# Last feed-forward chunks reordered (four up products, then three down products), and the weight of the final norm multiplied in earlier

## What is computed

```python
h = h + merged @ w_out
hid = causal_dwconv(rms_norm(h, ffn_norm_g) @ w_ffn_up, ffn_conv_w, ffn_conv_b)   # width 3
g_ff, up = jnp.split(hid, 2, axis=-1)                                            # 2816 each
h = h + (jax.nn.silu(g_ff) * up) @ w_ffn_down                                    # 2816 -> 1024
out = h * lax.rsqrt(jnp.mean(h * h, axis=-1, keepdims=True) + 1e-6) * final_norm_g
```

## Time and profile before

| | us |
|---|---|
| median of 3 runs | 727.36 |
| the profiled execution's own time | 725.45 |
| its span, first to last instruction | 723.6 |
| TensorE busy in the span | 694.6 (96%) |
| VectorE busy | 495.7 (69%) |
| ScalarE busy | 372.6 (51%) |
| GpSimd busy | 14.9 (2%) |

### The profile page before, as it was taken

The page is one execution under the profiler, slowest core; times in us unless marked ns, Lnnn a source line. Parts: engine busy times, 40 slices in busy tenths (PEclk is TensorE's granted clock), DMA queues, the critical chain, the costliest instruction groups (busy, mean ns, idle before and its releaser), DMA issues.

```text
span 723.6 us, 13986 instructions
## 1 busy us (share of the span) xinstructions
PE 694.6 (96%) x5478; PEld 676.2 (93%) x5478; DVE 495.7 (69%) x626; ACT 372.6 (51%) x469; POOL 14.9 (2%) x26
## 2 busy tenths in 40 slices
PE   5898889999999999999999999999999999999994
PEld 5898889999999999999999999999999999999993
DVE  4893798878775656766754445655668777777784
ACT  5544787767663445454443333442465555455531
POOL 0000000000010000000000000000000000000021
PEclk9999999999999999999999999999999999999997
DMA  8729784739635544335555755556546555555511
GB/s 251 218 60 316 232 259 135 252 117 301 192 117 175 174 153 138 118 117 173 175 175 176 232 174 175 174 175 212 166 134 212 178 175 188 204 186 174 174 58 58
DMA packets 118170, 127.90 MB, mean 177 GB/s; under 512 B 4302, under 2 KB 113279, under 8 KB 117631
## 3 DMA queue, kind: packets, MB, share of 16 engines
q1 hardware_dynamic: 118143, 127.54, 55.0%
HBM read 126.43 MB, written 2.67 MB: 178 GB/s over the span
## 4 chain that ended last, share of the span: by engine, by line
PE 82%; DVE 8%; DMA 3%; ACT 2%; issue 2%; SPq 2%; DVEq 0%; POOL 0%; POOLq 0%; ACTq 0%
PE ps L339 26%; PE ps L341 26%; PE ps L340 26%; DVE w_lo L311 3%; DMA acs_b<-acs_d 2%; DVE conv_a L1214 2%; DMA w_raw<-w_in 1%; DVE conv_g L1497 1%; PE ps L626 1%; ACT decay L920 1%; PE ps L645 0%; PE ps L661 0%; PE ps L611 0%; PE ps L654 0%; DVE conv_o L1221 0%
## 5 line engine op out<-in xcount | busy, mean ns | idle before, releaser
L339 PE MATMUL ps<-tok_hi,w_hi 128*128 128x256 f32 x1056 | 302.7, 287 | 4.9 <-DVE w_lo L311 4.2
L341 PE MATMUL ps<-tok_hi,w_lo 128*128 128x256 f32 x1056 | 300.4, 284 | 0.0
L340 PE MATMUL ps<-tok_lo,w_hi 128*128 128x256 f32 x1056 | 300.3, 284 | 0.0
L311 DVE TENSOR_TENSOR w_lo<-w_raw,w_hi 128x2048 fp32r<-128x2048 f32 x107 | 244.8, 2289 | 73.4 <-ACT w_hi L307 73.2
L307 ACT ACTIVATE w_hi<-w_raw 128x2048 fp32r<-128x2048 f32 x108 | 206.2, 1910 | 58.5 <-PE ps L341 43.4
L339 PEld LDWEIGHTS ps<-tok_hi,w_hi 128*128 128x128 f32 x1056 | 204.3, 193 | 7.5 <-DVE w_lo L311 4.6
L340 PEld LDWEIGHTS ps<-tok_lo,w_hi 128*128 128x128 f32 x1056 | 204.3, 193 | 0.4
L341 PEld LDWEIGHTS ps<-tok_hi,w_lo 128*128 128x128 f32 x1056 | 204.2, 193 | 0.0
L339 PE MATMUL ps<-os_hi,w_hi 128*128 128x256 f32 x128 | 36.3, 284 | 0.0
L341 PE MATMUL ps<-os_hi,w_lo 128*128 128x256 f32 x128 | 36.2, 283 | 0.0
L340 PE MATMUL ps<-os_lo,w_hi 128*128 128x256 f32 x128 | 36.2, 283 | 0.0
(11 more groups left out here) (274 smaller groups left out, 1154.5 us busy)
## 6 DMA issues: line engine op xcount, KB each, us to landing
w_raw<-w_in SPq DMA_DIRECT2D x95, 512.0 KB, 4.8
w_raw<-w_ffn_up SPq DMA_DIRECT2D x44, 512.0 KB, 4.4
w_raw<-w_ffn_down SPq DMA_DIRECT2D x22, 512.0 KB, 4.0
w_raw<-w_mem_kv SPq DMA_DIRECT2D x16, 512.0 KB, 4.0
w_raw<-w_br_ssm SPq DMA_DIRECT2D x16, 512.0 KB, 4.3
acs_b<-acs_d SPq DMA_DIRECT2D x4, 1024.0 KB, 7.0
w_raw<-w_br_attn SPq DMA_DIRECT2D x8, 512.0 KB, 4.4
w_raw<-w_br_mem SPq DMA_DIRECT2D x8, 512.0 KB, 4.1
```

The source lines that it names most:

```text
L311: dve.tensor_tensor(w_lo[:, s, :], w_raw[:, s, :], w_hi[:, s, :].bitcast(F32), ALU.subtract).then_inc(lo_ready[s], 1)
L339: pe.matmul(o, a[0], b[0], start=start, stop=False, **kw)
L340: pe.matmul(o, a[0], b[1], start=False, stop=False, **kw)
L341: return pe.matmul(o, a[1], b[0], start=False, stop=stop, **kw)
```

## The change

The last two chunks (9 and 10) are taken out of the loops. The order on TensorE after chunk 8's step becomes gate 9, up 9, gate 10, up 10, down 8, down 9, down 10. The blocks are loaded in the same sequence of slots as before; what is in four of them differs. `ffn` of chunk 10 reads its gate product from slot 2 and its up product from slot 0. Chunk 9's hidden parts go to `last_hi` and `last_lo`, chunk 10's to two new tiles `end_hi` and `end_lo`, at places in memory that are free by then. The last down block is split by VectorE, between `hid` and `end_lo`, and GpSimd's split is gone.

In the final norm VectorE multiplies each quarter by the weight right after its addition, into `h_sc` (four new instructions), while ScalarE squares into a tile of its own (`junk_y`). GpSimd has three small instructions for each row tile in place of four. The last multiplication is by the column alone: VectorE does the right half of each row tile and ScalarE the left half. VectorE's first such multiplication stands after the third quarter and ahead of the fourth addition. ScalarE's first stands after the second square and ahead of the third. The right half is written out first.

```diff
--- before.py
+++ after.py
@@ -64,6 +64,7 @@
 BIAS_W = 3 * P
 
 RA, RB, RC, RD, RE, RF, RG = 0, 8, 12, 16, 20, 24, 26
+RL = RG + F_STEPS - 2
 DT_STEPS = 19
 
 
@@ -206,6 +207,9 @@
     gain_fin = place("gain_fin", R + 44, [D])
     last_hi = place("last_hi", R + 20, [2, T], F32R)
     last_lo = place("last_lo", R + 22, [2, T], F32R)
+    end_hi = place("end_hi", R + 48, [2, T], F32R)
+    end_lo = place("end_lo", R + 50, [2, T], F32R)
+    junk_y = place("junk_y", R + 52, [NT, D // 2])
     rstd_b = place("rstd_b", R + 18.5, [T])
     pad_g = place("pad_g", R + 0, [2, FTAPS - 1 + T])
     pad_u = place("pad_u", R + 2.25, [2, FTAPS - 1 + T])
@@ -272,8 +276,8 @@
               "h_lo"))
     pads_zero, conv_begun, f_step, g_tanh, g_silu, hid_done, hid_hi_s, hid_lo_s = map(
         sem, ("pads_zero", "conv_begun", "f_step", "g_tanh", "g_silu", "hid_done", "hid_hi_s", "hid_lo_s"))
-    down_done, y_added, y_sumsq, y_var, y_rstd, y_scaled, y_out = map(
-        sem, ("down_done", "y_added", "y_sumsq", "y_var", "y_rstd", "y_scaled", "y_out"))
+    down_done, y_added, y_gained, y_sumsq, y_var, y_rstd, y_left, y_right, y_out = map(
+        sem, ("down_done", "y_added", "y_gained", "y_sumsq", "y_var", "y_rstd", "y_left", "y_right", "y_out"))
 
 
     def load(sp, r, s, w, col):
@@ -530,16 +534,22 @@
 
             load(sp, RF + 1, 1, w_ffn_up[0], 0)
             load(sp, RF + 1, 2, w_ffn_up[0], FFN)
-            with sp.Fori(1, F_STEPS) as f:
+            with sp.Fori(1, F_STEPS - 2) as f:
                 r = f + (RG - 1)
                 load(sp, r, 0, w_ffn_up[0], CW * f)
                 load(sp, r, 1, w_ffn_up[0], FFN + CW * f)
                 load_down(sp, r, 2, f - 1)
-            load_down(sp, RG + F_STEPS - 1, 0, F_STEPS - 1)
-            for n in range(2 * NT):
-                t = n // 2
-                sp.wait_ge(y_scaled, n + 1)
-                sp.dma_start(out[0, t * P:(t + 1) * P, halfcols(n)], h_sc[:, t, halfcols(n)]).then_inc(y_out, 16)
+            load(sp, RL - 1, 0, w_ffn_up[0], CW * (F_STEPS - 2))
+            load(sp, RL - 1, 1, w_ffn_up[0], FFN + CW * (F_STEPS - 2))
+            load(sp, RL - 1, 2, w_ffn_up[0], CW * (F_STEPS - 1))
+            load(sp, RL, 0, w_ffn_up[0], FFN + CW * (F_STEPS - 1))
+            load_down(sp, RL, 1, F_STEPS - 3)
+            load_down(sp, RL, 2, F_STEPS - 2)
+            load_down(sp, RL + 1, 0, F_STEPS - 1)
+            for t in range(NT):
+                for n, done in ((1, y_right), (0, y_left)):
+                    sp.wait_ge(done, t + 1)
+                    sp.dma_start(out[0, t * P:(t + 1) * P, halfcols(n)], h_sc[:, t, halfcols(n)]).then_inc(y_out, 16)
             sp.wait_ge(y_out, 16 * 2 * NT)
 
 
@@ -829,18 +839,29 @@
                     mm.then_inc(h_spread, 1)
                     for b in range(4, 8):
                         open_bank(pe, b)
-            with pe.Fori(1, F_STEPS) as f:
+            def down(r, s, n, hi, lo):
+
+                pe.wait_ge(hid_lo_s, n)
+                pe.wait_ge(lo_ready[s], r + 2)
+                down_part(pe, s, 0, hi, lo)
+                down_part(pe, s, 1, hi, lo).then_inc(gemm_done[s], 1)
+
+            with pe.Fori(1, F_STEPS - 2) as f:
                 r = f + (RG - 1)
                 gemm_cols(pe, r, 0, tok_hi, tok_lo)
                 gemm_cols(pe, r, 1, tok_hi, tok_lo)
-                pe.wait_ge(hid_lo_s, f)
-                pe.wait_ge(lo_ready[2], r + 2)
-                down_part(pe, 2, 0, hid_hi, hid_lo)
-                down_part(pe, 2, 1, hid_hi, hid_lo).then_inc(gemm_done[2], 1)
+                down(r, 2, f, hid_hi, hid_lo)
+            gemm_cols(pe, RL - 1, 0, tok_hi, tok_lo)
+            gemm_cols(pe, RL - 1, 1, tok_hi, tok_lo)
+            pe.wait_ge(bank_free[2], RF + 3)
+            gemm_cols(pe, RL - 1, 2, tok_hi, tok_lo, free=())
+            gemm_cols(pe, RL, 0, tok_hi, tok_lo)
+            down(RL, 1, F_STEPS - 2, hid_hi, hid_lo)
+            down(RL, 2, F_STEPS - 1, last_hi, last_lo)
             pe.wait_ge(hid_lo_s, F_STEPS)
-            pe.wait_ge(lo_ready[0], RG + F_STEPS + 1)
+            pe.wait_ge(lo_ready[0], RL + 3)
             for t in range(NT):
-                down_part(pe, 0, t, last_hi, last_lo, down_done)
+                down_part(pe, 0, t, end_hi, end_lo, down_done)
 
 
         @block.scalar
@@ -1067,9 +1088,10 @@
             split_hi(act, RG, 0)
 
 
-            def ffn(f, sa, ra, sb, rb, after_gate, after_up, last, first=False, final=False):
-                for n, (s, r, pad, conv, tile) in enumerate(((sa, ra, pad_g, conv_g, 0), (sb, rb, pad_u, conv_u, FT))):
-                    act.wait_ge(bank_free[s], r + 2)
+            def ffn(f, sa, na, sb, nb, after_gate, after_up, last, first=False, hi=hid_hi):
+                for n, (s, freed, pad, conv, tile) in enumerate(((sa, na, pad_g, conv_g, 0),
+                                                                 (sb, nb, pad_u, conv_u, FT))):
+                    act.wait_ge(bank_free[s], freed)
                     if not first:
                         act.wait_ge((g_silu, hid_done)[n], f)
                     for j in range(2):
@@ -1083,22 +1105,30 @@
                         act.wait_ge(f_step, 8 * f + 4)
                         act.activation(tanh_g[:], conv_g[:], ACT.Tanh).then_inc(g_tanh, 1)
                 act.wait_ge(hid_done, f + 1)
-                if not first and not final:
+                if not first and hi is hid_hi:
                     act.wait_ge(gemm_done[2], f + RG)
-                act.activation((last_hi if final else hid_hi)[:], hid[:], ACT.Copy).then_inc(hid_hi_s, 1)
+                act.activation(hi[:], hid[:], ACT.Copy).then_inc(hid_hi_s, 1)
                 for rr, ss in last:
                     split_hi(act, rr, ss)
 
-            ffn(0, 1, RF + 1, 2, RF + 1, [(RG, 1)], [(RG, 2)], [], first=True)
-            with act.Fori(1, F_STEPS - 1) as f:
+            ffn(0, 1, RF + 3, 2, RF + 3, [(RG, 1)], [(RG, 2)], [], first=True)
+            with act.Fori(1, F_STEPS - 2) as f:
                 r = f + (RG - 1)
-                ffn(f, 0, r, 1, r, [(r + 1, 0)], [(r + 1, 1)], [(r + 1, 2)])
-            r = RG + F_STEPS - 2
-            ffn(F_STEPS - 1, 0, r, 1, r, [(r + 1, 0)], [], [], final=True)
+                ffn(f, 0, r + 2, 1, r + 2, [(r + 1, 0)], [(r + 1, 1)], [(r + 1, 2)])
+            ffn(F_STEPS - 2, 0, RL + 1, 1, RL + 1, [(RL, 0)], [(RL, 1)], [], hi=last_hi)
+            ffn(F_STEPS - 1, 2, RF + 4, 0, RL + 2, [(RL, 2)], [(RL + 1, 0)], [], hi=end_hi)
             for n in range(2 * NT):
+                t = n // 2
                 act.wait_ge(y_added, n + 1)
-                act.activation(h_sc[:, n // 2, halfcols(n)], h_nat[:, n // 2, halfcols(n)], ACT.Square,
+                if n > 1:
+                    act.wait_ge(y_sumsq, n - 1)
+                act.activation(junk_y[:, n % 2, :], h_nat[:, t, halfcols(n)], ACT.Square,
                                accum_out=stat[:, 6 + n:7 + n]).then_inc(y_sumsq, 1)
+                if n % 2:
+                    act.wait_ge(y_gained, n + 1)
+                    act.wait_ge(y_rstd, t + 1)
+                    act.activation(h_sc[:, t, halfcols(0)], h_sc[:, t, halfcols(0)], ACT.Copy,
+                                   scale=stat[:, 6 + n:7 + n]).then_inc(y_left, 1)
 
 
         @block.vector
@@ -1477,7 +1507,7 @@
             dve.wait_ge(pads_zero, 2)
 
 
-            def ffn(f, sa, ra, sb, rb, early, after_gate, after_up, final=False):
+            def ffn(f, sa, ra, sb, rb, early, after_gate, after_up, hi=hid_hi, lo=hid_lo):
 
                 def pad_with(s, r, pad, splits):
                     dve.wait_ge(gemm_done[s], r + 1)
@@ -1512,26 +1542,38 @@
                 for rr, ss in after_up:
                     split_lo(dve, rr, ss)
                 dve.wait_ge(hid_hi_s, f + 1)
-                hi, lo = (last_hi, last_lo) if final else (hid_hi, hid_lo)
                 dve.tensor_tensor(lo[:], hid[:], hi[:].bitcast(F32), ALU.subtract).then_inc(hid_lo_s, 1)
 
             ffn(0, 1, RF + 1, 2, RF + 1, [(RG, 0)], [(RG, 1)], [])
-            with dve.Fori(1, F_STEPS - 1) as f:
+            with dve.Fori(1, F_STEPS - 2) as f:
                 r = f + (RG - 1)
                 ffn(f, 0, r, 1, r, [(r, 2)], [(r + 1, 0)], [(r + 1, 1)])
-            r = RG + F_STEPS - 2
-            ffn(F_STEPS - 1, 0, r, 1, r, [(r, 2)], [], [], final=True)
-            for n in range(2 * NT):
+            ffn(F_STEPS - 2, 0, RL - 1, 1, RL - 1, [(RL - 1, 2)], [(RL, 0)], [(RL, 1)], last_hi, last_lo)
+            ffn(F_STEPS - 1, 2, RL - 1, 0, RL, [], [(RL, 2)], [(RL + 1, 0)], end_hi, end_lo)
+
+            def add_down(n):
+
                 dve.wait_ge(down_done, n + 1)
                 part = h_nat[:, n // 2, halfcols(n)]
                 dve.tensor_tensor(part, ps[:, 4 + n, :], part, ALU.add).then_inc(y_added, 1)
+                dve.wait_ge(y_added, n + 1)
+                dve.tensor_tensor(h_sc[:, n // 2, halfcols(n)], part, gain_fin[:, halfcols(n)],
```

(29 more changed lines are left out.)

## The result

The changed kernel takes 719.88 us (median of 4 runs, 719.74 to 721.55) beside 727.3 for the kernel before in the same comparison: ratio 0.9912, interval 0.9896 to 0.9928. The profiled execution took 719.74 with a span of 718.0, where the sum had said 718.3. So the two profiles differ by 5.6 us, and the two medians by 7.4. Most of the study is about those two numbers: where the 5.6 came from, and why the medians said more.

What follows compares the result with a forecast made beforehand. TensorE carries 82% of the chain, with gains only near its end and in the serial norm behind it. Gains of 4.81, 0.60 and 0.55 less a 0.70 loss made 5.26 us off 727.36, so 722.1, range 721.0 to 724.2.

Steps and rivals of the forecast that it cites:

- the sum: Whole span: 723.6 - 4.81 + 0.70 - 0.60 - 0.55 = 718.3 us, so 5.26 off.
- taking the same 5.26 off 727.36: Last step: the span's gain taken off the median shown, 1.9 above the profiled execution, giving 722.1 us.
- The range's upper end: Forecast's slow limit, 724.2 us, said to go up through rival 2's gap and half of its low clock.
- waiting and low clock of TensorE: Before and in the last down product: 3.09 us of waiting and 1.72 of low clock go, gain 4.81.
- fourth addition late: Final norm: GpSimd's power and a column multiplication put the fourth addition at 712.15, not 711.45; loss 0.70 us.
- from it to the last multiplications: Final norm, fourth addition to `y_rstd`: 2.46 us in place of 3.06, one instruction fewer; gain 0.60.
- from those to the last issue: End of the norm: VectorE's and ScalarE's halves run at once, last issue at 0.88 after 1.43; gain 0.55 us.
- Rival 2: Before down 9 or down 10: wait moved, gap of 1.0 gives 723.1 us, with low clock 724.8; chance 0.13.
- the margins: Ahead of down 9 and down 10: inputs ready 0.9 and 1.0 us before TensorE wants them.
- rival 1: Final norm: GpSimd's one-column power doesn't hold VectorE up, everything after 0.33 earlier, 721.8 us; chance 0.20.
- the straight line: Norm's multiplication by a column on VectorE: 0.48 us, between 0.35 at 256 columns and 0.75 at 1024.
- Part 1: Order on TensorE in the last chunks: with the new sequence TensorE never waits and the clock stays up; 4.81 us gain.

Runs made afterwards that it cites:

- fill_gap: Kernel before with 12 matmuls of no use in the gap ahead of its last down product; 725.39 us, ratio 0.9986.
- pool_split: Changed kernel with the last down block split by GpSimd again, new order and new norm kept; 722.31 us, ratio 0.9947.
- fourth_first: Changed kernel with the fourth addition ahead of VectorE's first column multiplication and all four squares ahead of ScalarE's first; 721.23 us, ratio 0.9924.
- early_split: Kernel before with the last weight block split by VectorE ahead of `pad_u`, where it waits for TensorE; old order and norm; 723.25 us, ratio 0.9957.
- norm_only: Kernel before with only the new final norm, old order and GpSimd's split kept; 724.87 us, ratio 0.9984.
- peel_only: Kernel before with its last two feed-forward steps written out behind the loops, in the old order; 725.44 us, ratio 0.9987.
- warm_old: Kernel before with 8 and 10 matmuls of no use in two early gaps of TensorE; 727.13 us, ratio 1.0012.

## Why the prediction was right and wrong

**The step that failed is the last one of the sum**: "taking the same 5.26 off 727.36". The 5.26 were right within 0.4, the base was not. The text itself noted that the profiled execution stood 1.9 us below the median, and I took the distance as fixed. With 61 runs it is 1.0 (725.45 against 726.43), and three runs are a draw from a band 3 us wide; so were the four of the result. Neither the forecast nor the range, whose lower end of 721.0 held only what I did not know of the change itself, had any room for that. From the better base, 726.43, the same sum gives 721.2, against 720.28 as the median and 720.74 as the mean of the changed kernel's 16 runs.

Counted in means, the 2.2 us between 722.1 and 719.88 are 1.00 of base (727.36 against 726.36), 0.86 of the result's own draw (719.88 against 720.74) and 0.36 that the sum was short of (5.62 against 5.26). So the base is the largest part and not all of it: even the mean of 16 runs lies under 721.0. The range's upper end adds up to 724.0 (723.1 and half of 1.72), not 724.2; nothing hung on it.

Term by term, measured in the two profiles:

| term | forecast | measured |
|---|---|---|
| waiting and low clock of TensorE | 4.81 | 4.86 |
| fourth addition late | -0.70 | -0.41 |
| from it to the last multiplications | 0.60 | 0.43 |
| from those to the last issue | 0.55 | 0.43 |
| last issue to the end | 0 | 0.16 |
| ahead of the tail | 0 | 0.13 |
| sum | 5.26 | 5.60 |

Up to the last issue the four priced terms come to 5.31 against 5.26. That is closer than the terms deserve: +0.05, +0.29, -0.17 and -0.12 cancel. The last issue to the end, 2.85 before and 2.69 after, can't be credited to the change, since it varied from 2.41 to 2.92 under the old norm.

- TensorE: 715.84 - 684.15 against 710.85 - 684.02. Rival 2's gap did not come: the margins were 1.1 and 1.3 us. By `fill_gap`, 1.61 of the 4.86 were low clock, not 1.72, and the other 3.25 the wait and what goes with it, not 3.09.
- The fourth addition, at 711.68 where 711.27 was possible: rival 1 was right. The third multiplication started at 710.68 inside GpSimd's power (710.52 to 711.07) and still took 0.69. What the Trainium skill's rule says of two SBUF inputs (SBUF — State Buffer, "Who interferes with whom"), that VectorE stands while GpSimd reads SBUF, holds for the large split, 6.03, and 6.10 in `pool_split`; of a one-column operation that started first, VectorE felt nothing, and here the measurement decides.
- The third row of the table. The rule did show the other way round: GpSimd's small instruction at 712.59, inside VectorE's multiplication of 712.40 to 713.09, took 0.56 where the one at 708.83 took 0.19, and the next one started at 713.32, 0.1 late. The prediction looked only at the instruction behind the fourth square and found no multiplication in its way; this was the one behind the third square, which ScalarE's left half (711.16, 0.72 long) had made late. In `fourth_first`, where that left half stands behind the squares, it took 0.19 and the next one was not late. That is most of what the third row lacks.
- The last multiplications: VectorE 0.48, as by the straight line of the earlier trace rows; ScalarE 0.72, priced at 0.63 as its square.
- Part 1's explanation was right in its direction and incomplete. I named GpSimd's split as why the chunk was late and then gave the whole gain to the order. `early_split` shows that 3.72 of the 4.85 up to the last issue (4.16 of 5.27 by the tails) are to be had without the order.

## What to carry to other kernels

Ask of a gap first whether its chain is long by its own steps or stretched by a neighbour: here one split on GpSimd made VectorE 4.3 us late, and moving it into a place where VectorE waited anyway gave 3.72 of the 4.85 us that this move and a reordering of seven products gave together. When a forecast starts from a few runs, their spread belongs into its range even if every term is exact; a distance inside the trace, from an instant ahead of the edit to the last DMA's issue, repeated within 0.03 us and showed the 0.35 and 0.46 of two edits, where medians over 6 to 12 runs could hardly tell 1. Taken to the end of the span it does not: there the same code differed by 0.4.

## Unexpected in the hardware

Gaps of 0.76 and 1.52 us before the last product left the clock at 1.00 behind them, one of 1.88 was followed by 0.66 over four us, and the one of 2.93 by low clock in all four profiles that have it (before, `norm_only`, `peel_only`, `warm_old`). Elsewhere the gap's length did not decide: one of 2.53 at 66 us in the kernel before was not followed by low clock, and of the two at 100 us, 2.45 in the kernel before and 2.44 in `warm_old`, only the second was. Each of these is one execution.

The last 256 KB DMA took 2.41 to 2.92 us from its issue to the end of the span in seven profiles where nothing differs in it.
